# Two Strassen-style projections: seven half products in three PSUM places, copied by ScalarE and added by VectorE

## The reference

```python
hn = _rmsnorm(x, pre_g).astype(x.dtype)
proj = jnp.einsum('bld,de->ble', hn, w_in).astype(F32)     # 1072 tokens x 1024 -> 8200 (A), 6160 (C)
q, k, v, og, ig, fg, z, xr, gr = _split(proj, EVEN_SPLITS) # layer A; layer C: q, k, v, r, alow
...
hm = jax.nn.sigmoid(og) * hm
hm = _head_norm(hm, m_norm_g, M_HEADS) * jax.nn.silu(z)
...
o = (_head_norm(o, g_norm_g, G_HEADS) * jax.nn.silu(r)).astype(x.dtype)
```

## Time and profile before

| | |
|---|---|
| median of 3 runs | 2098.28 us (2097.23 to 2099.08) |
| the profiled execution | 2098.2 us |
| its span | 2096.4 us |
| PE busy | 2027.8 us, 97% |
| DVE, ACT, POOL busy | 1239.6, 798.4, 320.3 us |
| pairs of projection A | 354.0 to 687.7 us |
| pairs of projection C | from 1304.6 to about 1638 us |
| DVE additions at L657 | 220 of 0.71 us, 110 in each projection |

### The profile page before, as it was taken

The page is one execution under the profiler, slowest core; times in us unless marked ns, Lnnn a source line. Parts: engine busy times, 40 slices in busy tenths (PEclk is TensorE's granted clock), DMA queues, the critical chain, the costliest instruction groups (busy, mean ns, idle before and its releaser), DMA issues. The chain is left out here.

```text
span 2096.4 us, 33284 instructions
## 1 busy us (share of the span) xinstructions
PE 2027.8 (97%) x12862; PEld 1803.7 (86%) x12862; DVE 1239.6 (59%) x2206; ACT 798.4 (38%) x1501; POOL 320.3 (15%) x442
## 2 busy tenths in 40 slices
PE   7999999999999799999979999999999799999998
PEld 7999999999999677787659999999999677777774
DVE  5466676645564666666646557676655465455544
ACT  5555543323231544444345344332212343333323
POOL 0000000000000532242210000000000452323222
PEclk9999999999999999999979999999999899999999
DMA  3121232443333754555332332444433544545442
GB/s 141 56 63 51 65 103 76 149 155 93 114 102 102 244 175 161 173 166 190 102 133 76 98 88 84 139 137 134 117 95 112 181 173 165 183 164 182 161 155 73
DMA packets 211496, 268.92 MB, mean 128 GB/s; under 512 B 49396, under 2 KB 157172, under 8 KB 209304
## 3 DMA queue, kind: packets, MB, share of 16 engines
q1 hardware_dynamic: 211352, 266.95, 39.9%
HBM read 172.72 MB, written 94.18 MB: 127 GB/s over the span
## 5 line engine op out<-in xcount | busy, mean ns | idle before, releaser
L657 DVE TENSOR_TENSOR pa_stage<-pa_ps,pa_stage 128x536 f32<-128x536 f32 x110 | 77.0, 712 | 119.3 <-PE pa_ps L624 111.0
L657 DVE TENSOR_TENSOR pc_stage<-pc_ps,pc_stage 128x536 f32<-128x536 f32 x110 | 77.0, 712 | 100.4 <-PE pc_ps L624 79.3
L471 PE MATMUL pa_ps<-a_XT_hi,pa_w_hi 128*128 128x358 f32 x576 | 133.2, 340 | 0.3 <-PEq L204 0.3
L471 PE MATMUL pa_ps<-a_XT_hi,pa_w_lo 128*128 128x358 f32 x576 | 125.9, 327 | 0.0
L471 PE MATMUL pa_ps<-a_XT_lo,pa_w_hi 128*128 128x358 f32 x576 | 125.8, 326 | 0.0
L624 PE MATMUL pc_ps<-c_XT_hi,pc_w_hi 128*128 128x268 f32 x384 | 110.2, 287 | 0.0
L624 PE MATMUL pa_ps<-a_XT_hi,pa_w_lo 128*128 128x268 f32 x384 | 110.1, 287 | 0.0
L624 PE MATMUL pc_ps<-c_XT_hi,pc_w_lo 128*128 128x268 f32 x384 | 110.1, 287 | 0.0
L624 PE MATMUL pc_ps<-c_XT_lo,pc_w_hi 128*128 128x268 f32 x384 | 110.1, 287 | 0.0
L624 PE MATMUL pa_ps<-a_XT_lo,pa_w_hi 128*128 128x268 f32 x384 | 110.0, 286 | 0.0
L624 PE MATMUL pa_ps<-a_XT_hi,pa_w_hi 128*128 128x268 f32 x384 | 109.8, 286 | 0.0
(11 more groups left out here) (581 smaller groups left out, 6000.8 us busy)
## 6 DMA issues: line engine op xcount, KB each, us to landing
pa_w_raw<-in_w_a SPq DMA_DIRECT2D x57, 512.0 KB, 4.6
pc_w_raw<-in_w_c SPq DMA_DIRECT2D x49, 512.0 KB, 4.5
scr_c<-pc_stage SPq DMA_DIRECT2D x48, 512.0 KB, 3.2
scr_a<-pa_stage SPq DMA_DIRECT2D x40, 512.0 KB, 3.2
mc_sample_state<-in_s SPq DMA_DIRECT2D x32, 512.0 KB, 4.6
out_s_s<-mc_sample_state SPq DMA_DIRECT2D x32, 512.0 KB, 2.8
ma_sample_state<-in_c SPq DMA_DIRECT2D x32, 257.0 KB, 4.1
out_c_s<-ma_sample_state SPq DMA_DIRECT2D x32, 257.0 KB, 2.6
```

The source lines that it names most:

```text
L471: ins = pe.matmul(self.ps[:, 3 * s + t, 0:TC], w[:, k, :], x[:, k, t * TC:(t + 1) * TC], start=(k == 0 and j == 0), stop=(k == KT - 1 and ...
L657: dve.tensor_tensor(dst, self.out(p, product), x, ALU.add).then_inc(self.added, 1)
```

## The change

Three places of two banks replace four. Products 1, 6, 7 and 4 of a pair go into one place, each accumulated onto what is there; 5 and 3 share a second; 2 has the third. The places of {1, 6, 7, 4} and of 2 swap from pair to pair. A partial sum is read in between: ACT copies after 1, 6, 5 and 4 to the four quarters, DVE adds after 2, 7 and 3. So a pair has four copies on ACT and three additions on DVE, in place of one and seven. Since the next product adds onto the same place, PE waits for the read of the product before it in that place. The order of products becomes 1265734, in pair 0 5126374. The order of work on ACT and DVE is rewritten (`act_pair`, `dve_pair`), and the tables of C and A are loaded one pair later.

```diff
     def order(self, p):
-        return "1265374" if p else "5412637"
+        return "1265734" if p else "5126374"
...
-        s = (self.at(p, product) + 1) % 4
+        s = {1: p % 2, 6: p % 2, 7: p % 2, 4: p % 2, 2: 1 - p % 2, 5: 2, 3: 2}[product]
...
+        opens = product in (1, 2, 5)
...
-                    ins = pe.matmul(bank[:, half, :], a[:, k, :], b[:, k, cols], start=(k == 0 and j == 0),
-                                    stop=(k == KH - 1 and j == 2))
+                    ins = pe.matmul(bank[:, half, :], a[:, k, :], b[:, k, cols], start=(opens and k == 0 and j == 0),
+                                    stop=(k == KH - 1 and j == 2), skip_group_check=True)
...
+            if name == "1":
+                if p:
+                    self.wait_added(pe, p - 1, 2)
+                else:
+                    pe.wait_ge(self.G.psum_free[0], (self.first + 1) // 2)
+            elif name == "2":
+                if p:
+                    self.wait_copied(pe, p - 1, 4)
+            elif name == "6":
+                self.wait_copied(pe, p, 1)
+            elif name == "5":
+                if p:
+                    self.wait_added(pe, p - 1, 3)
+            elif name == "7":
+                self.wait_copied(pe, p, 6)
+            elif name == "3":
+                self.wait_copied(pe, p, 5)
+            else:
+                self.wait_added(pe, p, 7)
...
+        dst, s = {1: (upper[0], 0), 6: (upper[1], 0), 5: (lower[1], 1), 4: (lower[0], 1)}[product]
+        act.wait_ge(self.spilled[s], 32 * (self.before + p))
         act.wait_ge(self.done, self.at(p, product))
         act.activation(dst, self.out(p, product), ACT.Copy).then_inc(self.copied, 1)
...
+        dst, copied = {2: (upper[0], 1), 7: (lower[1], 5), 3: (upper[1], 6)}[product]
+        self.wait_copied(dve, p, copied)
         dve.wait_ge(self.done, self.at(p, product))
+        dve.tensor_tensor(dst, self.out(p, product), dst, ALU.add).then_inc(self.added, 1)
...
+    def act_pair(self, act, p, tiles, more, finish, after_first=lambda: None, late=lambda: None):
         if p:
+            self.split_lower_hi(act, p)
+            finish(p - 1, 1)
+            self.copy(act, p, 1, tiles)
+            after_first()
+        else:
+            self.copy(act, p, 1, tiles)
+            self.copy(act, p, 5, tiles)
+        if more:
+            self.split_upper_hi(act, p + 1)
+        self.copy(act, p, 6, tiles)
+        if p:
+            self.copy(act, p, 5, tiles)
+        late()
+        if more:
+            self.split_sums_hi(act, p + 1)
+        finish(p, 0)
+        self.copy(act, p, 4, tiles)
+        if not more:
+            finish(p, 1)
+
+    def dve_pair(self, dve, p, tiles, more, finish, middle=lambda: None):
+
+        if p:
+            self.split_sums_lo(dve, p)
             self.split_lower_lo(dve, p)
+            finish(p - 1, 1)
+        self.add(dve, p, 2, tiles)
+        middle()
+        if more:
+            self.sum_weights(dve, p + 1)
+        if p:
+            self.add(dve, p, 7, tiles)
+        if more:
             self.split_upper_lo(dve, p + 1)
...
+        self.add(dve, p, 3, tiles)
+        if not p:
+            self.add(dve, p, 7, tiles)
+        finish(p, 0)
+        if not more:
+            finish(p, 1)
```

More of the change, by code:

```diff
@@ L645, in products, with copy, add, wait_tile @@
             self.product(pe, p, int(name))
-    def copy(self, act, p, product, dst):
+    def copy(self, act, p, product, tiles):
+        upper, lower = tiles
+        dst, s = {1: (upper[0], 0), 6: (upper[1], 0), 5: (lower[1], 1), 4: (lower[0], 1)}[product]
+        act.wait_ge(self.spilled[s], 32 * (self.before + p))
         act.wait_ge(self.done, self.at(p, product))
         act.activation(dst, self.out(p, product), ACT.Copy).then_inc(self.copied, 1)
-    def add(self, dve, p, product, dst, x, after):
+    def add(self, dve, p, product, tiles):
+        upper, lower = tiles
+        dst, copied = {2: (upper[0], 1), 7: (lower[1], 5), 3: (upper[1], 6)}[product]
+        self.wait_copied(dve, p, copied)
         dve.wait_ge(self.done, self.at(p, product))
-        if after:
-            dve.wait_ge(self.added, 7 * p + after)
-        dve.tensor_tensor(dst, self.out(p, product), x, ALU.add).then_inc(self.added, 1)
+        dve.tensor_tensor(dst, self.out(p, product), dst, ALU.add).then_inc(self.added, 1)
+    def wait_tile(self, eng, p, m):
+        self.wait_added(eng, p, (3, 7)[m])
+        self.wait_copied(eng, p, (6, 4)[m])
+        if m == 0:
+            self.wait_added(eng, p, 2)
     def t_sums(self, dve, i):
@@ L723, in t3_lows @@
         dve.sem_inc(self.t_ready, 1)
[L725 to L739, removed]
-        if p:
-            self.split_lower_lo(dve, p)
[L742 to L759, removed]
-            self.split_upper_lo(dve, p + 1)
[L761 to L769, removed]
@@ L1027, in _ @@
                         if kind == "v":
-                            spill(HP.added, HP.ready(p)[m], m, h, A_SLOT[kind] + m)
+                            HP.wait_tile(sp, p, m)
+                            spill(HP.done, 7 * p + 6 + m, m, h, A_SLOT[kind] + m)
                         else:
@@ L1128, in finish @@
                         return
[L1129 removed]
+                    HP.wait_tile(act, p, m)
                     if kind == "k":
@@ L1138, in _ @@
                     more = p + 1 < NPAIR
-                    if p == 3 * H:
+                    if p == 3 * H + 1:
                         act.preload_act_table_set('natural_log_exp_and_others')
[L1141 to L1145, removed]
-                    if more:
-                        HP.split_lower_hi(act, p + 1)
-                    finish(p, 1)
+                    HP.act_pair(act, p, (upper, lower), more, finish)
             @block.vector
@@ L1258, in _ @@
                 for p in range(NPAIR):
[L1259 to L1262 removed]
+                    HP.dve_pair(dve, p, (upper, lower), p + 1 < NPAIR, z_gate)
             @block.gpsimd
@@ L2549, in _ @@
                     else:
-                        spill(HP.added, HP.ready(p)[0], 0, h, 4 + d)
-                        spill(HP.added, HP.ready(p)[1], 1, h, 5 + d)
+                        for m in range(2):
+                            HP.wait_tile(sp, p, m)
+                            spill(HP.done, 7 * p + 6 + m, m, h, 4 + d + m)
             @block.scalar
@@ L2689, in _, with gate @@
                 HP.t3_lows(dve)
-                def gate(p, m, x):
+                def gate(p, m):
                     gated, h, d = head_of(p)
+                    if not gated:
+                        return
+                    x = flat[m]
                     dve.wait_ge(sig_ready, 2 * p + m + 1)
@@ L2701, in _ @@
                 for p in range(NPAIR):
-                    if p and head_of(p - 1)[0]:
-                        gate(p - 1, 1, flat[1])
-                    HP.sums_of(dve, p, upper, lower, p + 1 < NPAIR, (lambda: gate(p, 0, flat[0])) if head_of(p)[0] else (lambda: None))
+                    HP.dve_pair(dve, p, (upper, lower), p + 1 < NPAIR, gate)
             @block.tensor
```

51 lines of the change are left out of this document (16 added, 35 removed).

## The result

The changed kernel takes 2123.01 us (median of 4 runs, 2121.49 to 2124.87) against 2098.45 us for the kernel before (4 runs, 2097.23 to 2099.08): the ratio is 1.0118, with an interval of 1.0101 to 1.0136. It is slower by 24.6 us. The prediction was 2119.5 us in a range of 2106 to 2128, so direction and range held; 3.5 us are missing from the sum. The profiled execution took 2124.87 us, its span is 2123.1 us, 26.7 us more than before.

What follows compares the result with a forecast made beforehand. PE, busy without a gap in both projections, was taken as the bound; new PE waits of 11.0 (gated pairs), 6.3 (start of A) and 4.0 us (start of C) sum to 21.3 on 2098.2, giving 2119.5 us, range 2106 to 2128.

Steps and rivals of the forecast that it cites:

- Gated pairs: Pairs 9 to 12 in A, 2 to 8 in C: PE waits 1.0 us each for copy 6, 11.0 us.
- the chain: In gated pairs: product 3, sums, sigmoid, DVE's multiplications, spill, load, high part, then copy 6 at 12.75 to 13.0 us.
- 12.75 − 11.90: Gated pairs: PE's restart behind copy 6 at 12.75 (to 13.0) us into the pair, against product 7 due at 11.90.
- the load is early enough: Rival, 17%: loads land in 3.5 us or the chain is 1 us shorter; only the starts cost, 2108.5 us.
- Start of A: First pair of projection A: waits of 2.7, 2.2 and 1.4 us before products 6, 7 and 4, together 6.3 us.
- Start of C: First pair of projection C: waits before products 1, 6 and 4 (0.9, 2.5, 1.0), less 0.4, together 4.0 us.
- the sum is made without it: The 21.3 us sum leaves out any cost of a clock drop after the waits at the starts.
- Rule and row: By the skill's rule start A costs more than its waits; rows show clock drops, but not amid dense work.
- the clock falls: Rival, 10%: PE's clock drops to 1.2 GHz in the start waits, 1.6 us each, two to four drops, 2124 us.
- DVE's lighter load: Both projections: DVE 88 us less, ACT 57 us more, both beside PE, so 0 on the path.
- Matmuls speed up: Rival, 4%: fewer PSUM reads by DVE make PE's matmuls faster; 6 ns each gives 2087 us.
- Reading and adding on: In all pairs: accumulating onto a place that was read costs nothing extra, bounds 0 and 0.

Runs made afterwards that it cites:

- the lower gate first: The change, with DVE multiplying the previous pair's lower tile ahead of the low part of the next lower tile: 2112.38 us, 1.0073 against the kernel before.
- Pair 0 in order: The change with copies 1 and 6 early and pair 0's additions, upper-tile finish and copy 4 ahead of next-pair work: 2101.63 us, 1.0010 against the kernel before.

## Why the prediction was right, and what it missed

**Gated pairs: right, in mechanism and size.** 11 waits by 1.0 were 11.0 us; the trace gives 12.2, and moving copy 6 alone removed 11.3. Every station of the chain was hit to some 0.1 us. That the last difference came out was more than the method warrants: the term was 12.75 − 11.90, and the earlier trace rows would have allowed landings that make it 0 or 16. The rival *the load is early enough* is what the lower gate first made of it, by 1.2 us.

**Start of A: right in the sum, not in its parts.** Predicted 6.3; with the gated waits gone A was +6.6. The waits were 2.5, 0.5 and 1.5 (2.7, 2.2 and 1.4 predicted), since the fall of the clock ate most of the second: product 7 is set by the load. The step that costed the three waits one by one came out only because the load of the upper tile fixes when product 7 can start, so that the first two waits share one sum. I did not say so.

**Start of C: the mis-sized term.** Predicted 4.0; with the gated waits gone C was +6.2. Product 1 waited 0.7 to 1.2 us idle (0.9 predicted), product 6 2.1 and product 4 0.9. With 0.27 of restart each and less the wait of before that is 4.3 in the run with +6.2, near the 4.0. The difference is the fall of the clock, 1.5 us of work, and some 0.4 of slower pairs. This is the step that failed: "the sum is made without it".

**Rule and row.** In these nine profiles, those of the change and of the eight runs, 20 of 29 waits between 1.86 and 2.95 us, all surrounded by dense work, were followed by a stretch at the lower level. The Trainium skill (TensorE: Matmul & The Clock Gate, Part 1) says that the clock is held down by default and released by activity, and its thin-M example has waits for data that lose it again and again. The traces agree with that: dense work around a wait did not prevent a fall. The rival *the clock falls*, 1.6 us a fall and 10% likely, had the price about right (1.5) and the chance much too low. It was not a rival to the mechanism but a term beside it. With 1.5 for C the sum is 21.3 + 1.5 = 22.8, 2121.0. The remaining 2.0 us to the median are the gated waits, 1.2 more than counted, and the pace of the pairs, 0.8; that this closes exactly is luck, since the four executions themselves spread over 3.4 us.

**DVE's lighter load: right, and worth nothing.** DVE fell by 81 us (88 predicted) and ACT rose by 48 (57), both beside PE. *Matmuls speed up* is refuted: v pairs take 20.86 us (658.23 to 679.09 for ACT's high part of the lower tile) where the earlier trace rows had 20.83, so they are no faster, though DVE reads PSUM far less.

**Reading and adding on: nearly free, not 0.** The bounds 0 and 0 were a little too tight. Pair 0 in order leaves +3 us over before, most of it in its three waits, but every pair is 0.02 to 0.03 us longer, 0.8 us in all. Whether that is the adding on or the new order of the products stays open.

What the change does give is room on DVE and an order with one place less in PSUM; this kernel gains nothing from either while PE is full.

## What to carry to other kernels

Fewer accumulator places turn slack into a chain: before costing the copy, read what stands ahead of it in its engine's queue, above all an operation that waits for a load, and put the copy first (or the load earlier). When one such wait is removed, ask at once what the next in the queue is, or the gain moves rather than comes. Where PE is full, add to each new wait of about 2 us or more half a chance or better of a fall of the clock, and ask whether something later, such as a load, covers it.

## What the hardware showed unexpectedly

A fall of the clock came in steps. None of the 70 waits of up to 1.69 us in the nine profiles was followed by one; of 29 between 1.86 and 2.95 us, 20 were, each with the clock short by 1.70 us, 1.5 us of work; all 3 of 4.44 to 4.90 us were, each with twice that. In the middle group length does not decide: 2.78 passed and 1.91 did not, and the same 2.5 us wait in A fell in four traces and passed in one. What does decide there stays open; no run tried to move a wait in time without changing it. The Trainium skill (TensorE: Matmul & The Clock Gate, Part 1) says that the activity monitor's window runs freely and is not tied to the kernel, by which the moment of a wait would count beside its length. The steps and the mixed middle group would agree with that, but nothing here shows it.
